# A hybrid decoder step on one core: the mLSTM's projection as three rounded products, and the order of loads and units in four other stages

## What is computed

```python
z = x @ w_in                        # q, k, v, o, gates of the mLSTM: 4*512 + 8 columns
logi, logf = gates[:4], log_sigmoid(gates[4:])
b = cumsum(logf); a = b + m_prev
mt = max(a, max(dmat))              # dmat: b[t] - b[s] + logi[s], causal
wts = exp(dmat - mt); inter = exp(a - mt)
num = inter * (q @ c_prev) + ((q @ k.T) * wts) @ v
h = num / max(abs(nq), exp(-mt))
c_new = inter[-1] * c_prev + (w_last * k).T @ v
...
ob = sum(softmax(lses) * outs)
x = layer_norm(ALPHA * x + concat([h * sigmoid(o), ob]) @ w_out)
x = layer_norm(ALPHA * x + square(relu(x @ w_up)) @ w_down)
```

## Time and profile before

| what | value |
|---|---|
| median of three executions | 3292.88 us (3292.0 to 3296.89) |
| the profiled execution | 3288.4 us |
| its span, first to last instruction | 3286.6 us |
| mean granted TensorE clock | 0.959 |
| TensorE busy | 3071.8 us, 93% |
| VectorE busy | 1561.1 us, 47% |
| ScalarE busy | 902.1 us, 27% |
| GpSimd busy | 195.0 us, 6% |
| the f32 projection of the mLSTM (L983) | 800 records, 248.7 us |
| the MLPs' hidden units (L2482) | 4608 passes, 1520.3 us |

### The profile page before, as it was taken

How to read it: one execution, slowest core, us unless ns; L and a number is a source line. 1 busy time by engine, 2 the same in 40 slices (tenths; PEclk the granted TensorE clock), 3 DMA queues, 4 the chain that set the end, 5 groups by cost and what they waited for, 6 DMA issues and landing times. The chain is left out here.

```text
span 3286.6 us, 46489 instructions
## 1 busy us (share of the span) xinstructions
PE 3071.8 (93%) x18199; PEld 2619.0 (80%) x18199; DVE 1561.1 (47%) x3277; ACT 902.1 (27%) x1905; POOL 195.0 (6%) x241
## 2 busy tenths in 40 slices
PE   8999699999996996999999999699797999999997
PEld 4666588788885875998999898588686899889986
DVE  1333543544435774344444446645554443444447
ACT  1222233333233433111121113444433111112113
POOL 0000000000000110100110010000000011001100
PEclk9999699999998997999999999899898999999999
DMA  6000231353788863110111011310421011101111
GB/s 212 20 19 16 52 130 45 113 202 132 262 262 282 284 220 109 52 51 29 48 51 51 26 64 43 119 38 28 152 87 39 26 51 51 51 26 51 51 38 68
DMA packets 134418, 300.09 MB, mean 91 GB/s; under 512 B 15048, under 2 KB 64392, under 8 KB 133192
## 3 DMA queue, kind: packets, MB, share of 16 engines
q1 hardware_dynamic: 134280, 298.19, 26.9%
HBM read 260.65 MB, written 93.34 MB: 108 GB/s over the span
## 5 line engine op out<-in xcount | busy, mean ns | idle before, releaser
L2482 PE MATMUL f_ps_u<-f_xT_hi,f_up_hi 128*128 128x384 f32 (+1 forms) x1536 | 507.9, 331 | 28.4 <-DVE f_up_lo L2637 12.1
L2482 PE MATMUL f_ps_u<-f_xT_hi,f_up_lo 128*128 128x384 f32 (+1 forms) x1536 | 506.3, 330 | 0.0
L2482 PE MATMUL f_ps_u<-f_xT_lo,f_up_hi 128*128 128x384 f32 (+1 forms) x1536 | 506.1, 329 | 0.0
L2652 DVE TENSOR_TENSOR f_hT_lo<-f_h,f_hT_hi 128x384 fp32r<-128x384 f32 (+1 forms) x192 | 146.1, 761 | 562.2 <-ACT f_hT_hi L2566 558.7
L2502 PE MATMUL f_ps_d<-f_dn_hi,f_hT_hi 128*128 128x512 f32 x1080 | 411.9, 390 | 1.3 <-DVE acc L2665 0.6
L2502 PE MATMUL f_ps_d<-f_dn_lo,f_hT_hi 128*128 128x512 f32 (+1 forms) x1080 | 411.7, 390 | 0.0
L2502 PE MATMUL f_ps_d<-f_dn_hi,f_hT_lo 128*128 128x512 f32 x960 | 373.9, 389 | 0.0
L2482 PEld LDWEIGHTS f_ps_u<-f_xT_hi,f_up_hi 128*128 128x128 f32 x1536 | 293.3, 191 | 31.2 <-issue 20.4
L2482 PEld LDWEIGHTS f_ps_u<-f_xT_lo,f_up_hi 128*128 128x128 f32 x1536 | 293.1, 191 | 1.1
L2482 PEld LDWEIGHTS f_ps_u<-f_xT_hi,f_up_lo 128*128 128x128 f32 x1536 | 292.8, 191 | 0.0
L2561 ACT ACTIVATE f_h<-f_ps_u 128x384 f32<-128x384 f32 (+1 forms) x192 | 91.0, 474 | 605.7 <-PE f_ps_u L2482 605.7
(11 more groups left out here) (458 smaller groups left out, 4510.3 us busy)
## 6 DMA issues: line engine op xcount, KB each, us to landing
w_group<-in_w_in_ab SPq DMA_DIRECT2D x9, 2048.0 KB, 15.6
sample_keys<-in_w_up SPq DMA_DIRECT2D x16, 1024.0 KB, 7.3
sample_keys<-in_w_down SPq DMA_DIRECT2D x16, 1024.0 KB, 5.0
wo<-in_w_up SPq DMA_DIRECT2D x16, 1024.0 KB, 7.4
wo<-in_w_down SPq DMA_DIRECT2D x16, 1024.0 KB, 5.0
out<-in_cache_dil_kv SPq DMA_DIRECT2D x8, 2016.0 KB
g_xn<-in_x_prompt SPq DMA_DIRECT2D x16, 512.0 KB, 4.3
sample_keys<-in_cache_dil_kv SPq DMA_DIRECT2D x8, 1024.0 KB, 7.7
```

Of the source, the lines that this page charges most:

```text
L2482: last = pe.matmul(ps_u[b % 3][:, 0:w], wp[:, k, f * P:(f + 1) * P], xp[:, k, t0:t0 + w], start=(k == 0 and q == 0), stop=(k == KT - 1 and ...
L2652: last = dve.tensor_tensor(hT[par][1][:, f, t0:end], hs[:, 0:end - t0], as32(hT[par][0][:, f, t0:end]), ALU.subtract)
```

## The change

In the mLSTM the weights are loaded in f32 into five raw buffers, rounded by ScalarE and their remainders taken by VectorE on the chip. The projection becomes three float32r passes for the prompt's tiles and two for the sample. x is rounded at its copy out of the transposes, and VectorE subtracts the remainder (`x_rest`). The x transposes move behind the first two projection chunks and are for the tile two ahead. The sample's buffers share memory with the raw weights, so C0 and the prefetch of the next stage's weights are issued, and GpSimd's clearing is done, when the last projection is complete. In the attention of layer 1, `x_rest` moves into the copies of the probabilities. In the layer 1 sample part, cache and mixes are loaded before the weights; in the layer 0 sample part the last mix is loaded earlier. In the MLPs four of group 0's down units run before group 1's hidden units, `ORDER` begins with two prompt tiles instead of the sample, and the first down weights are split earlier. The diff, cut:

```diff
-                    if n + 2 < N and not (swa and n < 0):
+                    if n + 2 < N and not (swa and (n < 0 or attends(n))):
                         x_rest(n + 2)
                     if attends(n):
                         for b in range(1, prob_banks(n), 2):
+                            if swa and b == min(5, prob_banks(n) - 1) and n + 2 < N:
+                                x_rest(n + 2)
                             dve.wait_ge(*banks.full(n, "p", b))
...
-                cfg["load_weights"](sp, range(2))
-                load(0, 1)
-                cfg["load_weights"](sp, range(2, NCH))
-                cfg["prefetch"](sp)
+                for c in range(NCH):
+                    cfg["load_weights"](sp, c, w_raw[c][:, :, :])
+                    if c == 1:
+                        load(0, 1)
...
+                def load_state():
+                    sp.wait_ge(z_full.sem, z_full.done(NT, NCH - 1))
+                    for k in range(4):
+                        sp.dma_start(C0[:, 2 * k:2 * k + 2, :, :].rearrange("p b h e -> p (b h) e"),
+                                     cfg["C0"][2 * k:2 * k + 2].rearrange("b h d e -> d (b h) e")).then_inc(loaded, 16)
+                    cfg["prefetch"](sp)
...
                         for k in range(KT):
-                            for out, a, b in z_parts(n, par, c):
-                                last = pe.matmul(out, xT[par][:, k, 0:out.shape[0]], W[:, k, a:b], start=(k == 0), stop=(k == KT - 1))
+                            hi, lo = w_high[c][:, k, :], w_low[c][:, k, :]
+                            if isinstance(n, int) and n == NT:
+                                passes = sample_passes(xT_hi[par][:, k, :], hi, lo, k == KT - 1)
+                            else:
+                                passes = [(*xw, P) for xw in split_passes((xT_hi[par][:, k, :], hi), (xT_lo[par][:, k, :], lo))]
...
-                    x_transposes(n, X_T, i + par, par ^ 1)
-                    pe.wait_ge(t_free.sem, t_free.done(n, X_T + 1))
+                    last_tile = isinstance(n, int) and n == LAST
+                    pe.wait_ge(t_free.sem, t_free.done(n, X_T + 1 - U))
                     project(n + 1, par ^ 1, (0, 1))
+                    if not last_tile:
+                        x_transposes(n, X_T, i + 1, par)
...
-                x_transposes(0, -2, 0, 0)
-                pe.wait_ge(t_free.sem, t_free.done(0, -1))
-                project(0, 0, range(NCH))
+                x_transposes(0, -4, 0, 0)
+                pe.wait_ge(t_free.sem, t_free.done(0, -3))
+                project(0, 0, (0,))
+                x_transposes(0, -2, 0, 1)
+                project(0, 0, range(1, NCH))
...
+                def round_weights(c):
+                    act.wait_ge(w_sems[c], 16)
+                    nc.scalar.copy(w_high[c][:, :, :], w_raw[c][:, :, :]).then_inc(w_hi, 1)
...
-                    x_out(n, X_T, par ^ 1)
-                    evacuate(n, C_T, tbank(par, C_T), cols[:, :], P)
+                    last_tile = isinstance(n, int) and n == LAST
+                    if not last_tile:
+                        x_out(n, X_T, par)
+                        act.wait_ge(t_free.sem, t_free.done(n, X_T + 1))
...
-                x_out(0, -2, 0)
+                x_out(0, -4, 0)
+                round_weights(0)
+                round_weights(1)
+                x_out(0, -2, 1)
+                for c in range(2, NCH):
+                    round_weights(c)
...
+                pool.wait_ge(z_full.sem, z_full.done(NT, NCH - 1))
+                pool.memset(s_rows[:, :], 0.0)
...
+                            if sample:
+                                s_link(dve.tensor_copy(dst, src[0:NS, a - lo:b - lo]))
+                                last = dve.tensor_tensor(dst, dst, src[NS:2 * NS, a - lo:b - lo], ALU.add)
...
+                def x_rest(n, c, par, sample=False):
+                    for half in range(2):
...
+                        dve.tensor_tensor(dst, bank[:, :].rearrange("p (k t) -> p k t", t=P)[:, :, 0:held],
+                                          xT_hi[par][:, ks, 0:held].bitcast(F32), ALU.subtract).then_inc(t_free.sem, 1)
+
+                def rest_of_weights(c):
+                    dve.wait_ge(w_hi, c + 1)
+                    dve.tensor_tensor(w_low[c][:, :, :], w_raw[c][:, :, :], w_high[c][:, :, :].bitcast(F32), ALU.subtract).then_inc(w_lo, 1)
...
                                       ALU.add).then_inc(masked.sem, 1)
+                    if not (isinstance(n, int) and n == LAST):
+                        x_rest(n, X_T, par, sample=isinstance(n, int) and n + 2 == NT)
                     z_out(n + 1, par ^ 1, (1,))
...
+                x_rest(0, -4, 0)
+                rest_of_weights(0)
                 dve.wait_ge(cleared, 3)
-                z_out(0, 0, range(NCH))
+                rest_of_weights(1)
+                x_rest(0, -2, 1)
+                z_out(0, 0, (0,))
+                for c in range(2, NCH):
+                    rest_of_weights(c)
+                    z_out(0, 0, (c - 1,))
+                z_out(0, 0, (NCH - 1,))
...
+                sp.dma_start(kv[:, :, :], cfg["cache"].rearrange("b s x h d -> s b (x h d)")).then_inc(kv_loaded, 16)
                 load_mix(0)
-                load_w(0)
-                sp.dma_start(kv[:, :, :], cfg["cache"].rearrange("b s x h d -> s b (x h d)")).then_inc(kv_loaded, 16)
-                load_w(1)
                 load_mix(1)
-                load_w(2)
+                for u in range(3):
+                    load_w(u)
...
+                    if n == BD:
+                        sp.wait_ge(*banks.full(NT - 1, "m", 1))
+                        for par in range(2):
+                            sp.wait_ge(ob_stored[par], 16 * HB * (BD // 2))
+                        load_mix(NT)
...
-ORDER = (NT,) + tuple(range(NT))
+ORDER = (0, 1, NT) + tuple(range(2, NT))
+EARLY = 4
...
-                def down(n, par):
+                def down(n, par, units=range(DN)):
                     pe.wait_ge(dn_lo.sem, dn_lo.done(n))
-                    pe.wait_ge(h_lo.sem, h_lo.done(n, UP - 1))
-                    for b in range(DN):
+                    pe.wait_ge(h_lo.sem, h_lo.done(n, UP - 1 if units[-1] >= EARLY else FT - 1))
+                    for b in units:
...
-                with pe.Fori(0, NFG // 2 - 1) as i:
+                down(0, 0, range(EARLY))
+                hidden(1)
+                down(0, 0, range(EARLY, DN))
+                hidden(2)
+                down(1, 1)
+                with pe.Fori(1, NFG // 2 - 1) as i:
...
+                    if b == 3:
+                        split_weights(0, dn_raw, dn[0], dn_loaded, None, dn_hi)
                 next_up(0)
-                split_weights(0, dn_raw, dn[0], dn_loaded, None, dn_hi)
...
+                    if b == 3:
+                        rest(0, dn_raw, dn, dn_hi, dn_lo)
                 rest(1, up_raw, up, up_hi, up_lo)
-                rest(0, dn_raw, dn, dn_hi, dn_lo)
```

More of the change, by code:

```diff
@@ L810, in mlstm @@
         xn = [sb(f"xn{i}", [P, D]) for i in range(2)]
-        xT = [sb(f"xT{i}", [P, KT, P]) for i in range(2)]
+        xT_hi = [sb(f"xT{i}_hi", [P, KT, P], F32R) for i in range(2)]
+        xT_lo = [sb("xT0_lo", [P, KT, P], F32R), cfg["xT_lo"]]
         z = [sb(f"z{i}", [P, 4 * WA]) for i in range(2)]
@@ L855, in mlstm @@
+        s_nq = sb_late("s_nq", [P, 6])
+        late.close()
+        with ExitStack() as first:
+            w_raw = [first.enter_context(nc.sbuf_tensor(f"m_w{c}_raw", [P, KT, W_AT[c]], F32)) for c in range(3)] + cfg["raw"]
+        w_low = [sb(f"w{c}_lo", [P, KT, W_AT[c]], F32R) for c in range(3)] + cfg["low"]
+        w_high = [sb(f"w{c}_hi", [P, KT, W_AT[c]], F32R) for c in range(NCH)]
         x_loaded = [sem(f"x_loaded{i}") for i in range(2)]
@@ L889, in tbank, with zbank @@
             return ps_t[(par * U + c) % 2] if c >= 0 else ps_t[c % 2]
[L891 to L895, removed]
-            mid = EDGES[c] + w // 2
-            return [(bank[0:NS, 0:w // 2], EDGES[c], mid), (bank[NS:2 * NS, 0:w // 2], mid, EDGES[c + 1])]
+        def zbank(par, c):
+            return ps_z[(par * NCH + c) % 2]
         def by_seq(t):
@@ L1013, in step @@
                     pe.matmul(ps_m[:, 12:16], ones[0:HA, :], ild[:, 0:HA], start=True, stop=True).then_inc(d_full.sem, 1)
-                    pe.wait_ge(t_free.sem, t_free.done(n, C_T, back=2))
-                    pe.transpose(tbank(par, C_T)[:, 0:P], rows[:, :], ident).then_inc(t_full.sem, 1)
+                    pe.wait_ge(t_free.sem, t_free.done(n, G_T) if last_tile else t_free.done(n, C_T, back=2))
+                    pe.transpose(tbank(par, C_T)[:, 0:P], rows[:, :], ident).then_inc(t_full.sem, 3 if last_tile else 1)
                     for h in range(HA):
@@ L1237, in z_out @@
                         dve.wait_ge(z_full.sem, z_full.done(n, c))
-                        for src, lo, hi in z_parts(n, par, c):
-                            held = src.shape[0]
```

(20 more changed lines are left out.)

126 lines of the change are left out of this document (73 added, 53 removed).

## The result

The changed kernel takes 3217.74 us (median of four executions, 3216.39 to 3218.59), the kernel before on the same chips 3294.89 (3292.0 to 3304.87): a ratio of 0.9762, 95% interval 0.9747 to 0.9776. The forecast was 3226 in a range of 3202 to 3254. The profiled execution of the changed kernel took 3216.39 us, with a span of 3214.6 against 3286.6: 72.0 less, where the sum had 66.6.

A forecast was written before the change was run, and what follows sets the result against it. TensorE, busy 93% of the span, was the bound. mLSTM -36.5, attention -7.5, layer 1 sample +0.5, layer 0 sample -8.3 and MLPs -14.8 sum to -66.6: from 3288.4 to 3221.8, median 4.5 above, so 3226; range 3202 to 3254.

The forecast's parts named there:

- The pass: mLSTM projection: a 412-column float32r pass costs 0.185 us, so 120 passes take 22.2 us, 5.4 less a tile.
- The step: mLSTM steps: -5.4 from passes, -1.7 from moved x transposes, +1.5 from C_T's wait; -5.6 each, -39 over seven.
- the clock's dips kept as they are: mLSTM steps: the forecast of -5.6 a step assumed TensorE's stretches at the low clock stay unchanged.
- The fourth rival: mLSTM steps: without the gap at the front, dips costing 20 us shrink by two thirds, giving 3213; chance 0.10.
- C_T and x: mLSTM step: transpose C_T waits for VectorE's subtraction, +1.5 us (0 to 3); x lands before its transposes.
- the slack of 1 us: mLSTM step: x lands 9.6 us after the step's start, its transposes come at 10.7.
- The start: mLSTM start: rounding and subtracting weights delay the first pass to about 19.5 and chunk 2; +5.5 us (3 to 8).
- The sample's state: mLSTM sample: C0 loads late, covered by VectorE's scans; counted as nothing, up to 10 us without that cover.
- The small edits: Attention of layer 1 -7.5, its sample projection +0.5, layer 0's sample and projection -8.3, the two MLPs -14.8 us.
- rival three: MLPs and layer 1 attention: early units wait for down weights, attention's wait moves; 14.8 + 7.5 back, 3248; chance 0.11.
- rival two: mLSTM keeps half its gain: x late, C_T waits twice as long or start costs 8; 3244; chance 0.14.
- The first rival: mLSTM projections: TensorE held at 1.2 GHz, 19 us more a tile, 150 over eight; 3376 in full; chance 0.05.

## Why the prediction was right, and where it was off

The time and its sign came out, from a sum whose largest term was 8 too small and whose others erred by up to 3 both ways. Stage by stage the misses are 13 us to the one side and 8 to the other; that they cancelled to 5 is luck.

**The pass.** 0.188 against 0.185 us; 120 of them 22.5 against 22.2. The line through two widths held. The Trainium skill ("FP8 and Floating Point Precision", section TensorE Precision Notes) counts a true f32 product as four passes. An estimate worked out from that, three quarters for three passes, is 20.7; the measurement is 1.8 us a tile above it.

**The step.** -5.6 was forecast with the dips kept. Without dips a step took 39.14 before (the spread in the kernel before) and 33.87 after (five steps of the changed kernel): -5.3. That is the work term, 7 x 5.3 = 37 of 47.5. Its parts erred a little: the passes gave 5.1 for 5.4, and the move of the x transposes 1.3 for 1.7 (3.7 less 1.4 and 1.0), because the 4.5 of the forecast held slow transposes of a dip. The step of the prediction that failed is "the clock's dips kept as they are": the other 10.5 are dips that went. The fourth rival priced that (20 us of dips, two thirds gone), but its reason, the gap at the front, is refuted: with the gap put back three of seven steps kept full clock, without it the clock fell at the start of all but one (0.95, the subtraction moved), and with it nothing fell behind spread products. The order of the one-column products decides whether the clock falls at a step's start. Whether it does, with the old order, differs from step to step and from kernel to kernel (0.99 in the changed kernel, 0.95 with the subtraction moved); by what rule stays open. The changed kernel's other executions have the same mean clock over the whole span, 0.968 to 0.969, and times within 2.2 us, so they can hardly have had many more dips than the profiled one. My 20 us for all the dips was too much, too: they cost 1.9 a step, 13 in seven. Part of the slow stretch lies in waits (TensorE stood idle in 1.0 of the 3.5 us from 169.80 on); what makes up the rest of the difference is not shown.

**C_T and x.** 1.38 against 1.5 in six steps, 1.1 in the seventh. x was there in time, as the slack of 1 us said.

**The start.** The sum, 47.7 against 42.4, was +5.3 and was put down as +5.5. The first pass at 19.59 was forecast to 0.1, and chunk 2 late as worked out. What I left out is that TensorE falls to the low clock in that wait: 18 passes 0.34 apart behind 34.13, 3 us. That is the difference of +8.3 to +5.5: where the clock didn't fall, in the run with the subtraction moved, the same start gave +5.4. The reordered start has it back, and 2.6 of the wait.

**The sample's state.** Its late loads cost nothing; the cover held. Of the 3.1 us gained there, 2.7 are "issue" waits (5.4 to 2.7), and they vary: that part took 43 to 54 us among the runs.

**The small edits.** Attention: -6.0 for -7.5; the waits fell by 6.6, and 4.2 are left where I left 3.3. Layer 1's sample part: 0.0 for +0.5, for the reason given, the key copies behind two roundings; moving them showed that the weights and the probabilities bind the stage past that. Layer 0's last mix: the wait of 5.8 and the slow stretch went in full; the stage gave 6.2 for 8.3 in this trace, and it moves by itself by as much as the difference. MLPs: -14.6 for -14.8; the early units fill the wait, with 0.4 each left for the down weights. So rival three is refuted, and rival two with it: the mLSTM gave 44, not half of its term.

**The first rival** had no part in it: the longest stretch of the projection at 1.2 GHz in the changed kernel's trace is the 6 us behind 34.13. The Trainium skill's loop that goes back to the low clock in every round ("TensorE: Matmul & The Clock Gate", section HAM oscillation) agrees with the step in kind: a stretch of little work at the end of each round, then slow passes. At the steps' starts it isn't a wait that does it here but narrow products; the dips around C_T, a wait of 1.4 us, are nearer to the skill's case.

## What to carry to other kernels

Price a new kind of pass by a line through two widths of it in the same trace. When a loop's clock is below 1, find what TensorE does just before the slow passes: here 24 one-column products in a row cost 1.9 us a step in the kernel before, and placing each beside a wide product with the same stationary operand took that away, there and in the changed kernel. It keeps a full clock; it doesn't bring a low one back (the last tile's products: 10.5 us at 0.50, against 7.1 in the old order). And when an operation is added to an engine that waits, put it before the wait: VectorE had 3.4 us free ahead of the mask, and the added subtraction stood behind it.

## What the runs showed of the hardware that I had not expected

Narrow products in a row let TensorE's granted clock fall although the engine is recorded as busy in them: before, 0.93 over seven steps with TensorE busy in 97% of the time; with the same instructions in another order, 1.00 in six of the seven. The order that kept the clock up also kept it down: once it had fallen at the start of the last tile's products, behind a wait of 4 us, the spread ones ran at 0.50 to their end, those in the old order at a mean of 0.75. The same instruction stream falls in some steps and not in others: in the run with the subtraction moved one step had 1.00 and 32.5 us, another 0.95 and 34.0. And a fall costs less than the clock that it takes: seven dipped steps lost 13 us, where a mean clock of 0.93 over 287 us would be 20.
